# First layer: the first query's product in the round of NSA's compression, and the memories' squares summed on GpSimd

## The chip, the cores and the metric

One core of one Trainium2 chip runs the whole program. The metric is the device time of one execution, in microseconds. Below, "products" are dense matrix products on TensorE, and "the remainder" of a weight is its low part, explained further down.

## What is computed

Two transformer blocks follow each other on 512 tokens of width 1024, in float32. The first block (`first_block`) is the one that the change is about:

```python
h = rms_norm(x, norm_in_g[l])
p = h @ w_in[l]                                  # rwkv | nsa | memory columns
y_rwkv = rwkv7_group(p_rwkv, ...)                # 8 heads of 64
y_nsa = nsa_group(p_nsa, pos, ...)               # 4 heads: compressed, selected, window
kv = rms_norm(mem, mem_norm_g[l]) @ w_mem_kv[l]
y_mem = memory_group(p_mem, mem_k, mem_v, ...)   # attention on 256 memory rows
x = x + concatenate([y_rwkv, y_nsa, y_mem]) @ w_out[l]
```

In `nsa_group` the keys and values `kcv` are cut in 31 windows of 32 rows, a position term is added, and a two-layer net compresses each window. Queries and the other keys are rotated (RoPE). The second block has an even mixer, an odd mixer, two cross attentions on another memory of 256 rows (`rms_norm(mem) @ wkv`, 16 column blocks each) and two MLPs.

## The kernel before, in words

**Products.** Activations lie transposed, 128 features by 512 tokens. A weight comes in units of 1024 rows by 128 columns, 512 KB. Each is split in a rounded part, made by ScalarE (`weight_hi`, L165), and a remainder, made by VectorE (`weight_lo`, L171, 1024 columns, it needs the rounded part). The activations are split the same way (L213, L218). `dense` (L189 and on) does 24 matmuls of 512 columns per unit. There are four raw buffers and three split ones: ScalarE prepares two units ahead of the one that is consumed, VectorE one ahead, in the order in which TensorE consumes units. SP loads unit n when the remainder of unit n-4 exists.

**The order of work.** Each engine has its own in-order program, written as generators. `first_layer` (L1437) weaves three lanes: rwkv 0 then rwkv 1; NSA, its heads 0 and 1, then rwkv 2 and 3 together; and, beside NSA, the memory and its heads. In one round each lane takes one step, rwkv first, then NSA, then memory. Each engine does its own part of each step, in this order, so whatever stands behind a waiting instruction on an engine waits too. Rounds are counted from 0:

- round 0: rwkv 0's key product; NSA's `kcv` product; the memory's first four tiles are split and squared
- round 1: LoRA products; NSA's compression, 64 matmul calls (128 instructions) of 64x31, on `kexp`, which VectorE builds by two adds (L1196) from the evacuated `kcv`; the memory's last four tiles
- round 2: the square sum kn of rwkv's key; NSA's q0 product; the memory's first key product, then the statistics of its norm. On VectorE the decay chain of rwkv stands ahead of NSA's step: two sigmoid forms, a scan, centring and differences (L956 to L975)
- round 3: rwkv's receptance product; rotation of q0, the compression's second layer (`c2`), q1's product; the second memory key
- rounds 4 and 5: one product by rwkv, one by NSA with the rotation of the one before, and a memory value
- later: NSA's gates, scores and heads; rwkv's inverse (masked products, six levels) and its four chunks. rwkv 2 and 3 begin at round 40; the layer has 76 rounds.

**Norm statistics.** ScalarE squares a tile (L226), VectorE adds it to a sum (L233); a matmul with ones sums over partitions. ScalarE rounds and squares in turns; the squares go through two buffers, so that from the fourth square on it waits for the addition two before (`square`, L222). For the memories a tile has 256 columns. In the cross layers `keys_vector` (L2023) has all eight tiles in one step, between the evacuation of one pair of query products and the next remainder. GpSimd is idle there; in the first layer it does six multiplies for each rwkv group (`rwkv_pool`).

Of the kernel before, what the change touches and what calls it, by code (L numbers as in the profile page):

```python
# [13 lines left out]
T = 512  # L14
# [206 lines left out]

def square(K, a, name, i, src, acc, tmp, scale=1.0):  # L222

    if i >= 3:
        a.wait_ge(*K.done("dve", *name, "sum", i - 2))
    a.activation(tmp[i % 2] if i else acc, src, ACT.Square, scale=scale).then_inc(*K.tell("act", *name, "sq", i))  # L226


def add_square(K, v, name, i, acc, tmp):
    v.wait_ge(*K.done("act", *name, "sq", i))  # L230
    if i:
        v.wait_ge(*K.own("dve"))
        v.tensor_tensor(acc, acc, tmp[i % 2], ALU.add).then_inc(*K.tell("dve", *name, "sum", i))  # L233


def stats_tensor(K, M, pe, name, acc, n=T, last=7, ones="ones"):
    b = K.take(*name, "ss")
    pe.wait_ge(*K.clear(*name, "ss"))
    if last:
        pe.wait_ge(*K.done("dve", *name, "sum", last))  # L240
# [245 lines left out]
def memory_split_scalar(K, M, a, name, mem, gname, hi, acc, tmp, which=range(ND)):  # L486
    for i in which:
        a.wait_ge(*K.landed(f"mem{i}", name[1] + 1))
        split_hi(K, M, a, name, i, mem[i], hi[i], M.PV(gname, i))
        square(K, a, name, i, mem[i], acc, tmp)  # L490


def memory_split_vector(K, M, v, name, mem, gname, hi, lo, acc, tmp, which=range(ND)):
    for i in which:
        split_lo(K, M, v, name, i, mem[i], hi[i], lo[i], M.PV(gname, i))
        add_square(K, v, name, i, acc, tmp)


def memory_tensor(K, M, pe, name, wname, n, hi, lo, acc, tmp):
    first = True  # L500
    for a in range(0, n, 2):
        for u in (a, a + 1):
            dense(K, M, pe, (*name, "k", u), wname, u, hi, lo, n=256, fresh=name if first else None)
            if first:
                stats_tensor(K, M, pe, name, acc, 256)
            first = False
# [95 lines left out]
def first_memory_vector(K, M, v):  # L602
    g = M.first
    for part in (range(4), range(4, ND)):
        memory_split_vector(K, M, v, M0, g.mem, "mem_norm_g", g.mem_hi, g.mem_lo, g.mem_acc, g.mem_tmp, part)
        yield
    yield from memory_vector(K, M, v, M0, 2, g.kap, g.mem_R, g.mem_vtmp)


def first_memory_scalar(K, M, a):  # L610
    g = M.first
    for part in (range(4), range(4, ND)):
        memory_split_scalar(K, M, a, M0, g.mem, "mem_norm_g", g.mem_hi, g.mem_acc, g.mem_tmp, part)
        yield
    yield from memory_scalar(K, M, a, M0, 2, g.vap, g.mem_R)
# [522 lines left out]
def nsa_tensor(K, M, pe):  # L1138
    s, hi, lo = M.nsa, M.hi[0], M.lo[0]
    dense(K, M, pe, ("kcv",), "w_in", 23, hi, lo)  # L1140
    yield
    pe.wait_ge(*K.landed("w1", 5))
    for z in range(2):
# [9 lines left out]
    yield  # L1153
    before = None
    for key, u, src in (("q0", 17, s.q[0]), ("q1", 18, s.q[1]), ("ks", 24, s.ks), ("kw", 25, s.kw), ("vsw", 26, s.tmp2)):
        if before is not None:
            rope_tensor(K, M, pe, *before)
        if key == "q1":
            b = K.take("c2")
# [27 lines left out]
def nsa_vector(K, M, v):  # L1187
# [5 lines left out]
    for half in range(2):  # L1193
        windows = s.kcv[:, half * 16:half * 16 + 496].rearrange("p (b r) -> p r b", b=31)
        pos = M.PV("pos", half * 16, 16).unsqueeze(2).to_broadcast([128, 16, 31])
        v.tensor_tensor(s.kexp[:, half * 496:half * 496 + 496].rearrange("p (r b) -> p r b", r=16), windows, pos,  # L1196
                        ALU.add).then_inc(*K.tell("dve", "kexp"))
    v.wait_ge(*K.done("pe", "cmp"))
    for z in range(2):
# [5 lines left out]
    K.also("dve", "cmp", 1, "silu")  # L1205
    before = None
    for key, src, dst in (("q0", s.q[0], s.qr[0]), ("q1", s.q[1], s.qr[1]), ("ks", s.ks, s.ks), ("kw", s.kw, s.kw),
                          ("vsw", s.tmp2, None)):
        if key == "q1":
            v.wait_ge(*K.landed("ncs", 2))  # L1210
        if before is not None:
            rope_vector(K, v, *before, s.cos, s.sin, s.tmp)
        if key == "q1":
            b = K.bank("c2")
# [56 lines left out]
def nsa_scalar(K, M, a):  # L1271
    s = M.nsa
    weight_hi(K, M, a)
    yield
    for z in range(2):
        silu_scalar(K, a, ("cmp", z, "h"), s.h[z][0:64, 0:31], s.h[z][0:64, 32:63])
    yield
    for key in ("q0", "q1", "ks", "kw", "vsw"):
        weight_hi(K, M, a)
# [733 lines left out]
def keys_vector(K, M, v, n, r):  # L2013
    s = M.cross
    queries_vector(K, M, v, n, 0, ("n", 2 + 3 * n))
    yield
    memory_split_vector(K, M, v, ("m", n + 1), s.mem, f"xa_mem{n}", M.mem_hi[1 - r], M.mem_lo[1 - r], s.acc, s.sq)
    queries_vector(K, M, v, n, 1)
# [212 lines left out]
def first_norms(K, M, v):  # L2231
    return (chain(idle(12), *(chain(idle(1), head_norms(K, v, nsa_heads(M, z)), idle(3)) for z in range(2))),
            chain(idle(6), *(chain(idle(1), head_norms(K, v, mem_heads(M, z)), idle(3)) for z in range(2))))
# [174 lines left out]
def build(nc, dram):  # L2408
    with ExitStack() as ctx:
# [19 lines left out]
        def halves(ts):  # L2429
# [19 lines left out]
            ("hi", 8), ("lo", 12)))  # L2449
        stats, g.mem_tmp = halves([tile("mem_stats", plain(1, 10))]), halves([tile("mem_sq", plain(1, 11))])  # L2450
        g.mem_acc, g.mem_R = stats
# [253 lines left out]
```

## Time and profile before

| | us |
|---|---|
| timed executions | 2149.06, 2160.72, 2165.86 |
| their median | 2160.72 |
| the profiled execution | 2146.59 |
| its span, first to last instruction | 2145.3 |
| TensorE busy in it | 2020.0 (94%) |
| VectorE, ScalarE, GpSimd busy | 1100.1, 872.5, 57.3 |

All durations below are of the profiled execution, and a sum made from them stands against its own time. The granted clock is a share of TensorE's full 2.4 GHz; 0.50 is the lower level, 1.2 GHz. A row of the timeline has start, length, engine, line, operation, output and inputs, and in brackets how long the engine had been idle and what released it. A length is that of the instruction; followers on the same engine can start before it ends. Engines: PE is TensorE, DVE VectorE, ACT ScalarE, POOL GpSimd.

### The profile page before, as it was taken

What the parts mean: (1) busy time and instruction counts of PE and PEld (TensorE: products, weight loads), DVE (VectorE), ACT (ScalarE), POOL (GpSimd) and SP (SyncE); (2) the same over time, 40 slices, a digit from 0 to 9 for tenths busy, and PEclk for the clock granted to TensorE, in tenths of its full rate; (3) what the DMA queues carried; (4) which work ended last, traced back from release to release, by engine and by line L of the source; (5) the groups of instructions that cost most, each with busy time, mean ns of one, the idle gap of its engine ahead of it and who ended that gap; (6) DMA issues with size and microseconds to landing.
All of it is one profiled execution on the core that took longest, in us unless ns stands there. A gap on an engine that the chain in (4) does not pass through costs nothing.

```text
span 2145.3 us, 28300 instructions
## 1 busy us (share of the span) xinstructions
PE 2020.0 (94%) x11400; PEld 1605.7 (75%) x11400; DVE 1100.1 (51%) x1921; ACT 872.5 (41%) x1567; POOL 57.3 (3%) x92
## 2 busy tenths in 40 slices
PE   6898888889999989999999999999999999999997
PEld 4776566768766669878888887667668978888886
DVE  5567567746466464454334344444565445343344
ACT  5325533244345354343223233565654344232232
POOL 0100012000000000000000000111000000000000
PEclk8989999999999999999999999999999999999999
DMA  5210011013211033222232322111123312322221
GB/s 203 88 50 21 20 59 49 3 60 112 79 59 40 20 118 128 69 89 99 89 105 91 98 99 79 60 50 60 49 79 120 107 59 96 101 98 89 99 98 69
DMA packets 54099, 169.63 MB, mean 79 GB/s; under 512 B 5777, under 2 KB 9425, under 8 KB 53969
## 3 DMA queue, kind: packets, MB, share of 16 engines
q1 hardware_dynamic: 53968, 167.82, 23.4%
q8 instruction: 92, 1.51, 0.3%
q14 instruction: 39, 0.31, 0.0%
HBM read 165.70 MB, written 2.10 MB: 78 GB/s over the span
## 4 chain that ended last, share of the span: by engine, by line
PE 62%; DVE 3%; ACT 2%; issue 1%; DMA 0%; SPq 0%; POOL 0%; DVEq 0%; ACTq 0%
PE ps L152 61%; PE ps L157 1%; DVE lo L1459 0%; DVE wr L171 0%; DVE X L1540 0%; DVE acc L233 0%; DVE X L1613 0%; DVE macc L233 0%; ACT hi L213 0%; ACT sa_sp L2195 0%; ACT sa_sp L2193 0%; ACT sb_sp L2195 0%; DMA raw<-d_sb_w_out 0%; ACT sb_sp L2198 0%; ACT wr L165 0%
## 5 line engine op out<-in xcount | busy, mean ns | idle before, releaser
L152 PE MATMUL ps<-hi,wr 128*128 128x512 f32 (+1 forms) x4616 | 1410.8, 385 | 52.1 <-DVE wr L171 34.7
L152 PEld LDWEIGHTS ps<-hi,wr 128*128 128x128 f32 x4616 | 861.4, 190 | 236.9 <-DVE wr L171 26.9
L152 PE MATMUL ps<-lo,wr 128*128 128x512 f32 (+1 forms) x2308 | 879.9, 381 | 0.0
L152 PEld LDWEIGHTS ps<-lo,wr 128*128 128x128 f32 x2308 | 439.1, 190 | 82.9 <-issue 3.4
L165 ACT ACTIVATE wr<-raw 128x1024 fp32r<-128x1024 f32 x293 | 307.8, 1053 | 360.4 <-PE ps L152 352.1
L171 DVE TENSOR_TENSOR wr<-raw,wr 128x1024 fp32r<-128x1024 f32 x293 | 361.2, 1233 | 4.3 <-ACT wr L165 2.3
L1524 DVE TENSOR_TENSOR X<-X,ps 128x512 f32<-128x512 f32 x80 | 55.0, 687 | 213.5 <-PE ps L152 213.5
L2078 ACT ACTIVATE mlp<-mlp 128x512 f32<-128x512 f32 x64 | 40.4, 632 | 208.1 <-DVE mlp L2061 208.1
L2061 DVE SCALAR_TENSOR_TENSOR mlp<-ps,R 128x512 f32<-128x512 f32 x64 | 44.3, 692 | 113.5 <-PE ps L152 106.5
L2064 DVE TENSOR_TENSOR lo<-mlp,hi 128x512 fp32r<-128x512 f32 x64 | 44.3, 692 | 87.5 <-ACT hi L2082 87.5
L213 ACT ACTIVATE hi<-X,pv 128x512 fp32r<-128x512 f32 x48 | 34.6, 721 | 98.8 <-DVE X L1524 78.4
L218 DVE SCALAR_TENSOR_TENSOR lo<-X,pv,hi 128x512 fp32r<-128x512 f32 x48 | 36.0, 749 | 32.1 <-ACT hi L213 32.1
L226 ACT ACTIVATE sq<-X 128x512 f32<-128x512 f32 x49 | 30.3, 618 | 28.9 <-DVE X L1524 28.9
L2082 ACT ACTIVATE hi<-mlp 128x512 fp32r<-128x512 f32 x64 | 40.4, 632 | 2.4
L233 DVE TENSOR_TENSOR acc<-acc,sq 128x512 f32<-128x512 f32 x50 | 34.6, 692 | 10.3 <-ACT sq L226 5.6
L432 ACT ACTIVATE x_pr<-ps,st 128x256 f32<-128x256 f32 x32 | 15.2, 475 | 60.6 <-DVE st L418 60.6
L2217 POOL TENSOR_SCALAR_AFFINE_SELECT sa_sp<-sa_sp 128x128 f32<-128x128 f32 x24 | 9.8, 409 | 1063.8 <-DVE sa_sp L2159 1063.8
L274 DVE SCALAR_TENSOR_TENSOR Y<-ps,R 128x512 f32<-128x512 f32 x16 | 11.1, 692 | 51.4 <-PE ps L152 48.1
L152 PE MATMUL ps<-x_pt,vt 128*128 128x128 f32 x256 | 34.3, 277 | 2.6 <-ACT x_pt L443 2.6
L152 PEld LDWEIGHTS ps<-x_pt,vt 128*128 128x128 f32 x256 | 32.3, 191 | 5.2 <-ACT x_pt L443 4.3
L152 PE MATMUL ps<-kt,Y 128*128 128x256 f32 x128 | 32.6, 379 | 0.0
L1459 DVE TENSOR_TENSOR lo<-Y,hi 128x512 fp32r<-128x512 f32 x40 | 24.7, 684 | 12.4 <-ACT hi L1453 12.4
(701 smaller groups left out, 1925.1 us busy)
## 6 DMA issues: line engine op xcount, KB each, us to landing
raw<-d_w SPq DMA_DIRECT2D x128, 512.0 KB, 3.4
raw<-d_wkv SPq DMA_DIRECT2D x32, 512.0 KB, 3.5
raw<-d_w_in SPq DMA_DIRECT2D x30, 512.0 KB, 3.5
raw<-d_sb_w_in SPq DMA_DIRECT2D x24, 512.0 KB, 3.4
raw<-d_ev_w_in SPq DMA_DIRECT2D x16, 512.0 KB, 3.5
raw<-d_wq SPq DMA_DIRECT2D x16, 512.0 KB, 3.5
raw<-d_wo SPq DMA_DIRECT2D x16, 512.0 KB, 3.4
X<-d_xT SPq DMA_DIRECT2D x16, 256.0 KB, 5.2
```

What stands on the lines that cost most here:

```text
L152: return pe.matmul(out, lhsT, rhs, start=start, stop=stop, skip_group_check=True)
L165: a.activation(M.wr[u % 3][:, 0:1024], M.raw[u % 4], ACT.Copy).then_inc(*K.tell("act", "hi", u))
L171: v.tensor_tensor(w[:, 1024:2048], M.raw[u % 4], w[:, 0:1024].bitcast(F32), ALU.subtract).then_inc(*K.tell("dve", "lo", u))
L213: a.activation(hi, src, ACT.Copy, scale=gcol).then_inc(*K.tell("act", *name, "hi", i))
L218: v.scalar_tensor_tensor(out=lo, in0=src, scalar=gcol, in1=hi.bitcast(F32), op0=ALU.mult, op1=ALU.subtract).then_inc(*K.tell("dve", *name, ...
L226: a.activation(tmp[i % 2] if i else acc, src, ACT.Square, scale=scale).then_inc(*K.tell("act", *name, "sq", i))
L233: v.tensor_tensor(acc, acc, tmp[i % 2], ALU.add).then_inc(*K.tell("dve", *name, "sum", i))
L1524: v.tensor_tensor(M.X[u], M.X[u], K.bank(*key, u), ALU.add).then_inc(*K.tell("dve", *key, u, frees=(*key, u)))
L2061: v.scalar_tensor_tensor(out=t, in0=K.bank(*key), scalar=0.0, in1=M.R, op0=ALU.max, op1=ALU.mult).then_inc(*K.tell("dve", *key, frees=key))
L2064: v.tensor_tensor(lo[u], t, hi[u].bitcast(F32), ALU.subtract).then_inc(*K.tell("dve", "h", n, q, "lo", u))
L2078: a.activation(t, t, ACT.Square).then_inc(*K.tell("act", *key, "sq"))
L2082: a.activation(hi[u], t, ACT.Copy).then_inc(*K.tell("act", "h", n, q, "hi", u))
```

## The change

Four things. (1) NSA's q0 product moves from round 2 to round 1, ahead of the compression's matmuls; q0's rotation and q1's product go to round 2, and every later NSA step, its heads, and rwkv 2 and 3 stand one round earlier. `c2` stays in round 3. (2) In the first layer's memory ScalarE does all eight roundings and then all eight squares in round 0, and VectorE does the eight remainders in round 1, behind `kexp` and a weight's remainder and ahead of q0's evacuation. (3) All sums of memory squares, here and in both cross layers, are added by GpSimd, at the front of its program, between rwkv's and the odd layer's operations, and at its end. The remainders stay on VectorE. (4) The first memory's squares go through four buffers in place of two; in the cross layers there are still two.

```diff
-def square(K, a, name, i, src, acc, tmp, scale=1.0):
-    if i >= 3:
-        a.wait_ge(*K.done("dve", *name, "sum", i - 2))
-    a.activation(tmp[i % 2] if i else acc, src, ACT.Square, scale=scale).then_inc(*K.tell("act", *name, "sq", i))
+def square(K, a, name, i, src, acc, tmp, scale=1.0, adds="dve"):
+    if i > len(tmp):
+        a.wait_ge(*K.done(adds, *name, "sum", i - len(tmp)))
+    a.activation(tmp[i % len(tmp)] if i else acc, src, ACT.Square, scale=scale).then_inc(*K.tell("act", *name, "sq", i))
...
-def memory_split_vector(K, M, v, name, mem, gname, hi, lo, acc, tmp, which=range(ND)):
+def memory_split_vector(K, M, v, name, mem, gname, hi, lo, which=range(ND)):
     for i in which:
         split_lo(K, M, v, name, i, mem[i], hi[i], lo[i], M.PV(gname, i))
-        add_square(K, v, name, i, acc, tmp)
+def memory_pool(K, g, name, acc, tmp):
+    for i in range(ND):
+        add_square(K, g, name, i, acc, tmp, "pool")
...
 def first_memory_vector(K, M, v):
     g = M.first
-    for part in (range(4), range(4, ND)):
-        memory_split_vector(K, M, v, M0, g.mem, "mem_norm_g", g.mem_hi, g.mem_lo, g.mem_acc, g.mem_tmp, part)
-        yield
+    yield
+    yield
...
 def first_memory_scalar(K, M, a):
     g = M.first
-    for part in (range(4), range(4, ND)):
-        memory_split_scalar(K, M, a, M0, g.mem, "mem_norm_g", g.mem_hi, g.mem_acc, g.mem_tmp, part)
-        yield
+    for i in range(ND):
+        a.wait_ge(*K.landed(f"mem{i}", 1))
+        split_hi(K, M, a, M0, i, g.mem[i], g.mem_hi[i], M.PV("mem_norm_g", i))
+    for i in range(ND):
+        square(K, a, M0, i, g.mem[i], g.mem_acc, g.mem_tmp, adds="pool")
+    yield
+    yield
...
     dense(K, M, pe, ("kcv",), "w_in", 23, hi, lo)
     yield
+    dense(K, M, pe, ("q0",), "w_in", 17, hi, lo)
     pe.wait_ge(*K.landed("w1", 5))
...
-    before = None
-    for key, u, src in (("q0", 17, s.q[0]), ("q1", 18, s.q[1]), ("ks", 24, s.ks), ("kw", 25, s.kw), ("vsw", 26, s.tmp2)):
-        if before is not None:
-            rope_tensor(K, M, pe, *before)
-        if key == "q1":
+    before = ("q0",), "rot_n", s.q[0], K.done("dve", "q0")
+    for key, u, src in (("q1", 18, s.q[1]), ("ks", 24, s.ks), ("kw", 25, s.kw), ("vsw", 26, s.tmp2)):
+        rope_tensor(K, M, pe, *before)
+        if key == "ks":
...
+    weight_lo(K, M, v)
+    g = M.first
+    memory_split_vector(K, M, v, M0, g.mem, "mem_norm_g", g.mem_hi, g.mem_lo)
+    evac(K, M, v, ("q0",), s.q[0], R)
     v.wait_ge(*K.done("pe", "cmp"))
...
     weight_hi(K, M, a)
     yield
+    weight_hi(K, M, a)
     for z in range(2):
         silu_scalar(K, a, ("cmp", z, "h"), s.h[z][0:64, 0:31], s.h[z][0:64, 32:63])
...
 def first_norms(K, M, v):
-    return (chain(idle(12), *(chain(idle(1), head_norms(K, v, nsa_heads(M, z)), idle(3)) for z in range(2))),
+    return (chain(idle(11), *(chain(idle(1), head_norms(K, v, nsa_heads(M, z)), idle(3)) for z in range(2))),
...
 def pool_program(K, M, g):
+    memory_pool(K, g, M0, M.first.mem_acc, M.first.mem_tmp)
     for i in range(4):
         rwkv_pool(K, g, i, M.rwkv[i])
+    memory_pool(K, g, ("m", 1), M.cross.acc, M.cross.sq)
     sb_layer(M, lambda z, L: sb_pool(K, g, z, L))
+    memory_pool(K, g, ("m", 2), M.cross.acc, M.cross.sq)
```

## Rows read from the trace of the kernel before

**Rows 1.** The page's engine line, then stages: length, busy, granted clock, DMA, GB/s.

```profile
PE 2020.0 (94%) x11400; PEld 1605.7 (75%) x11400; DVE 1100.1 (51%) x1921; ACT 872.5 (41%) x1567; POOL 57.3 (3%) x92
...
20.00:66.00 46.00, 37.43 (x243) 29.68 (x244) 27.48 (x61) 22.59 (x41) 0.00 (x0) 0.78 0.33 110
...
110.00:480.00 370.00, 325.11 (x3312) 245.32 (x3310) 237.45 (x534) 151.79 (x326) 21.79 (x18) 0.95 0.11 38
...
780.00:1600.00 820.00, 802.14 (x3803) 638.24 (x3802) 376.96 (x588) 351.37 (x610) 27.09 (x64) 0.99 0.25 83
```

**Rows 2.** Stages of TensorE alone in rounds 1 to 3: length, busy, granted clock.

```profile
36.50:41.40 4.90, 0.01 (x2) 0.71 0.00 2
41.40:48.40 7.00, 6.98 (x129) 0.50 0.01 2
48.40:56.80 8.40, 8.40 (x28) 0.77 0.01 2
56.80:59.70 2.90, 0.02 (x2) 0.89 0.00 0
59.70:65.40 5.70, 5.70 (x26) 0.50 0.36 113
65.40:71.10 5.70, 5.70 (x25) 0.96 0.46 152
```

**Rows 3.** Timeline of VectorE in rounds 0 to 2.

```profile
32.13 1.22 DVE L171 TENSOR_TENSOR wr<-raw,wr 128x1024 fp32r<-128x1024 f32 x1
35.49 0.69 DVE L277 TENSOR_TENSOR nsa_kcv<-ps,R 128x512 f32<-128x512 f32 x1 [2.14 <-PE ps L152]
...
39.39 1.89 DVE L1196 TENSOR_TENSOR nsa_kexp<-nsa_kcv,pv 128x496 f32<-128x496 f32 x2
...
53.19 0.42 DVE L956 TENSOR_SCALAR ra_sg<-ra_sg 128x512 f32<-128x512 f32 x1
...
58.38 1.21 DVE L171 TENSOR_TENSOR wr<-raw,wr 128x1024 fp32r<-128x1024 f32 x1
```

**Rows 4.** Timeline of TensorE: kn, and 32 small matmuls at either clock.

```profile
48.38 2.07 PE L152 MATMUL ps<-ra_tmp,cst 128*128 128x512 f32 x2
...
154.98 1.13 PE L152 MATMUL ps<-ra_Z,ra_X 64*64 64x64 f32 x32
...
159.21 0.69 PE L152 MATMUL ps<-ra_T,ra_S 64*64 64x64 f32 x32
```

**Rows 5.** Timeline of VectorE and GpSimd while both work.

```profile
79.45 2.05 DVE L171 TENSOR_TENSOR wr<-raw,wr 128x1024 fp32r<-128x1024 f32 x1
80.38 1.71 POOL L1112 TENSOR_TENSOR ra_kr<-ra_kk,ra_Sx 128x256 f32<-128x256 f32 x1
...
82.05 0.73 POOL L1114 TENSOR_TENSOR ra_kr<-ra_r,ra_S 128x256 f32<-128x256 f32 x1
...
82.21 1.66 DVE L171 TENSOR_TENSOR wr<-raw,wr 128x1024 fp32r<-128x1024 f32 x1
```

**Rows 6.** Cross layers: VectorE and TensorE's timeline at 790, then TensorE's stages.

```profile
788.77 0.87 DVE L218 SCALAR_TENSOR_TENSOR lo<-mem,pv,hi 128x256 fp32r<-128x256 f32 x2
...
795.65 1.22 DVE L171 TENSOR_TENSOR wr<-raw,wr 128x1024 fp32r<-128x1024 f32 x1
...
797.01 0.77 PE L152 MATMUL ps<-hi,wr 128*128 128x512 f32 x1 [3.44 <-DVE wr L171]
...
797.00:805.50 8.50, 8.49 (x25) 0.64 0.39 125
1624.20:1629.70 5.50, 5.50 (x25) 1.00 0.54 190
```

**Rows 7.** Rounds of rwkv 2 and 3: TensorE's waits, VectorE's timeline, a stage.

```profile
PE ps L152 <- DVE wr L171: 14.3, 3, 4.9
...
325.07 0.69 DVE L277 TENSOR_TENSOR ra_g<-ps,R 128x512 f32<-128x512 f32 x1 [3.21 <-PE ps L152]
...
341.79 1.21 DVE L171 TENSOR_TENSOR wr<-raw,wr 128x1024 fp32r<-128x1024 f32 x1
...
343.00:349.00 6.00, 5.85 (x14) 0.50 0.25 87
```

More of the change, by code:

```diff
@@ L219, in split_lo, with add_square, stats_tensor @@
                            op1=ALU.subtract).then_inc(*K.tell("dve", *name, "lo", i))
-def square(K, a, name, i, src, acc, tmp, scale=1.0):
-    if i >= 3:
-        a.wait_ge(*K.done("dve", *name, "sum", i - 2))
-    a.activation(tmp[i % 2] if i else acc, src, ACT.Square, scale=scale).then_inc(*K.tell("act", *name, "sq", i))
-def add_square(K, v, name, i, acc, tmp):
+def square(K, a, name, i, src, acc, tmp, scale=1.0, adds="dve"):
+    if i > len(tmp):
+        a.wait_ge(*K.done(adds, *name, "sum", i - len(tmp)))
+    a.activation(tmp[i % len(tmp)] if i else acc, src, ACT.Square, scale=scale).then_inc(*K.tell("act", *name, "sq", i))
+def add_square(K, v, name, i, acc, tmp, adds="dve"):
     v.wait_ge(*K.done("act", *name, "sq", i))
     if i:
-        v.wait_ge(*K.own("dve"))
-        v.tensor_tensor(acc, acc, tmp[i % 2], ALU.add).then_inc(*K.tell("dve", *name, "sum", i))
-def stats_tensor(K, M, pe, name, acc, n=T, last=7, ones="ones"):
+        v.wait_ge(*K.own(adds))
+        v.tensor_tensor(acc, acc, tmp[i % len(tmp)], ALU.add).then_inc(*K.tell(adds, *name, "sum", i))
+def stats_tensor(K, M, pe, name, acc, n=T, last=7, ones="ones", adds="dve"):
     b = K.take(*name, "ss")
@@ L239, in stats_tensor @@
     if last:
-        pe.wait_ge(*K.done("dve", *name, "sum", last))
+        pe.wait_ge(*K.done(adds, *name, "sum", last))
     else:
@@ L489, in memory_split_scalar @@
         split_hi(K, M, a, name, i, mem[i], hi[i], M.PV(gname, i))
-        square(K, a, name, i, mem[i], acc, tmp)
-def memory_split_vector(K, M, v, name, mem, gname, hi, lo, acc, tmp, which=range(ND)):
+        square(K, a, name, i, mem[i], acc, tmp, adds="pool")
+def memory_split_vector(K, M, v, name, mem, gname, hi, lo, which=range(ND)):
     for i in which:
         split_lo(K, M, v, name, i, mem[i], hi[i], lo[i], M.PV(gname, i))
-        add_square(K, v, name, i, acc, tmp)
+def memory_pool(K, g, name, acc, tmp):
+    for i in range(ND):
+        add_square(K, g, name, i, acc, tmp, "pool")
 def memory_tensor(K, M, pe, name, wname, n, hi, lo, acc, tmp):
@@ L504, in memory_tensor @@
             if first:
-                stats_tensor(K, M, pe, name, acc, 256)
+                stats_tensor(K, M, pe, name, acc, 256, adds="pool")
             first = False
@@ L1205, in nsa_vector @@
     K.also("dve", "cmp", 1, "silu")
[L1206 to L1213, printed above, removed]
+    v.wait_ge(*K.landed("ncs", 2))
+    before = ("q0",), s.q[0], s.qr[0]
+    for key, src, dst in (("q1", s.q[1], s.qr[1]), ("ks", s.ks, s.ks), ("kw", s.kw, s.kw), ("vsw", s.tmp2, None)):
+        rope_vector(K, v, *before, s.cos, s.sin, s.tmp)
+        if key == "ks":
             b = K.bank("c2")
@@ L1277, in nsa_scalar @@
     yield
-    for key in ("q0", "q1", "ks", "kw", "vsw"):
+    for key in ("q1", "ks", "kw", "vsw"):
         weight_hi(K, M, a)
@@ L2016, in keys_vector @@
     yield
-    memory_split_vector(K, M, v, ("m", n + 1), s.mem, f"xa_mem{n}", M.mem_hi[1 - r], M.mem_lo[1 - r], s.acc, s.sq)
+    memory_split_vector(K, M, v, ("m", n + 1), s.mem, f"xa_mem{n}", M.mem_hi[1 - r], M.mem_lo[1 - r])
     queries_vector(K, M, v, n, 1)
@@ L2449, in build @@
             ("hi", 8), ("lo", 12)))
-        stats, g.mem_tmp = halves([tile("mem_stats", plain(1, 10))]), halves([tile("mem_sq", plain(1, 11))])
+        stats, g.mem_tmp = halves([tile("mem_stats", plain(1, 10))]), halves([tile("mem_sq0", plain(1, 11)), tile("mem_sq1", plain(1, 13))])
         g.mem_acc, g.mem_R = stats
```

## The prediction

> **What bounds the kernel now.** The page comes first: TensorE is busy 94% of the span [rows 1], so a change pays only where TensorE stands still, runs at the lower clock, or gets less to do. Then the table by stages: the first layer's opening, 20 to 66 us, has 37.4 us of TensorE work in 46 us at a mean granted clock of 0.78; from 780 us on the kernel is nearly full [rows 1]. The opening is where this change works, so the next view is its table cut at TensorE's events [rows 2]. Read it as a story: 4.9 us of nothing, 7.0 us of compression matmuls at 0.50 (1.2 GHz), the square sum and q0's product while the clock comes back, 2.9 us of nothing, the first memory key at 0.50, and only at 65.4 the next product. VectorE's rows say who was late [rows 3]: kcv was evacuated at 35.5, but the two adds that build kexp start at 39.4 behind seven operations of the memory's first half; and the weight remainder for the memory key starts at 58.4 behind the decay chain that starts at 53.2. Last, in each of the two cross layers TensorE waits 3.4 us for a remainder, which stands behind fifteen memory operations, eight remainders and seven additions [rows 6].
>
> **Part 1, the order of the first rounds.** I follow TensorE from 36.5, when the two LoRA products end.
>
> q0's product needs weight unit 3, whose remainder was written from 32.1 on (1.22 us) [rows 3], so it starts at once and runs at the full clock: 5.7 us by the row 65.4 to 71.1 [rows 2], to 42.2. That fills the 4.9 us gap. VectorE meanwhile does kexp directly behind kcv: 36.2 plus 1.9, and up to 0.5 for each of the two adds if GpSimd stands in the way (part 2), 39.1 at the latest. So the wait for kexp is gone; it was worth 4.9 us, and what is late next is the clock.
>
> The compression: 128 matmul instructions, 7.0 us at 0.50 [rows 2]. There is no row of them at 2.4 GHz. Bounds: the block of 32 matmuls of 64x64 took 1.13 us at the lower clock and 0.69 at the full one [rows 4], so the best is 7.0 x 0.69/1.13 = 4.3; the worst is 7.0. Before, the clock had fallen inside the idle stretch and 7 us of these small matmuls did not bring it back [rows 2]; now they start at full clock and may lose it on the way. I take the middle, 5.6, ending at 47.8.
>
> Then kn and the rotation of q0 (kn took 2.1 at the lower clock [rows 4], so 1.1 at the full one; taken 1.6 each): 51.0. The rotation needs q0's evacuation on VectorE. In VectorE's queue that stands behind kexp, one remainder (1.2) and eight memory remainders (0.44 apart, 3.5): about 44 without, 46 with GpSimd's interference, hidden under the compression. q1's product needs unit 4, remaindered by then: 51.0 to 56.7, or 57.5 with a cold start.
>
> The memory key's product needs unit 5. Its remainder stands on VectorE behind: compression end 47.8, the copies 0.3, the decay chain with the two SiLUs 5.2 (53.2 to 58.4 in [rows 3]), and now also the rotation's three operations, 512 columns each like kcv's evacuation (2.1 together, formerly a round later). So it starts at 55.4 and ends at 56.6, and q1's product ends between 56.7 and 57.5: the 2.9 us gap closes, by little. The key's product with the statistics took 5.7 at 0.50 [rows 2]; at full clock about half, 2.9, with 0.6 for filling: from 57.1 to 60.7, against 65.4, a gain of 4.7. With a compression of 4.3 it is VectorE that is late (46.5 + 0.3 + 5.2 + 2.1 + 1.2 = 55.3, key done at 58.8, gain 6.6). With one of 7.0 and the cold 8.4 us for kn and a product that [rows 2] show, plus 2.1: 59.7, key done at 63.2, gain 2.2.
>
> At that point TensorE has also done a product and a rotation that used to come after it: 5.7 + 1.0 = 6.7 us less for the rest. All later NSA steps and heads stand one round earlier against rwkv 0 and 1, rwkv 2 and 3 likewise, and the layer has 75 rounds instead of 76. Rounds 3 to 5 keep their shape (a product by rwkv, one by NSA, one by the memory). Behind them the alignment changes: the rounds of the inverse are latency chains that NSA's matmuls fill, and the 6.7 us are kept only where TensorE is the late one. From 110 to 480 the layer has 45 us of idle TensorE in 370 [rows 1], 12%, and stalls shift rather than add. I keep 4.7 of the 6.7; bounds: nothing and all of it. One place I worked through, since the largest stalls are there, three waits for a remainder, 14.3 us in sum [rows 7]. Before, VectorE's queue between the gate's evacuation (325.1) and the wanted remainder (341.8) [rows 7] is 2.5 of masks, 9.1 of both decay chains, and 2.5 of masks; TensorE covers it with LoRA, kn, masked products and one product whose weights are ready. After, only one block of masks lies in that queue (2.5 less) but also one block of four products (2.2) and the LoRA pair (2.0) less of cover. It comes out 1.7 longer or so at one place, and this is inside the 2.0 I wrote off.
>
> ScalarE: its eight roundings and eight squares now stand together in front of kk2 and the two tanh. From 30.7: 8 x 0.40 + 8 x 0.33 = 36.5 without waits, 38.4 if the last squares wait for GpSimd; their reader is VectorE's decay chain, in round 2, no sooner than 46.5. Costed at nothing; if that cover were gone it would cost its 0.5 us. Loads: SP issues unit n when remainder n-4 exists; these remainders come earlier or at the same place, and the extra memory of the ring is in a tile of its own. Nothing is moved past a wait on SP.
>
> Part 1: 4.7 + 4.7 = 9.4 us, bounds 2.2 and 13.3.
>
> **Part 2, the squares' sums on GpSimd.** 21 additions of 128x256 leave VectorE (0.42 each, 0.44 in the queue) and go to GpSimd, where multiplies of this size took 0.73 alone and 1.71 beside VectorE [rows 5]. The rows show what the two do to each other. VectorE's remainder at 79.45 took 2.05 and that at 82.21 took 1.66 instead of 1.22; GpSimd's operation at 80.38 took 1.71 and ended 0.6 behind the end of VectorE's. While either works on two SBUF operands the other stands still. The Trainium skill, "GPSIMD Engine Reference", section 8 (Key points), says the same of instructions with two SBUF inputs; by that, and by these rows, the moved additions are not free to VectorE. Its section 4.1 (Engine selection) advises VectorE for elementwise adds, GpSimd being about two times slower; by that factor an addition would be 0.85 instead of the row's 0.73, and the sum below would change by some tenths.
>
> Cross layer, per layer [rows 6]: ScalarE's squares begin 3 us and more before VectorE is free for them, at 785, so GpSimd's chain can start at 786.2, well before VectorE's first memory remainder at 788.77 (it waits for a product's end). At 0.75 to 0.8 each, three to three and a half additions are done by then; the others alternate with VectorE's eight remainders. A turn of GpSimd costs VectorE what the lock costs beyond the overlap of dispatch, 0.45 to 0.5 (the remainder at 82.21 lost 0.44 to one addition-sized operation). New length of the block: 3.5 + 0.4 + 3 x 0.5 = 5.4, against 795.65 - 788.77 = 6.9: 1.5 us off a stall of 3.4. Bounds: 0.3 (GpSimd at 1.71 for each, sums queued behind, ScalarE's last rounding late) and 3.4 (all the stall). ScalarE's squares still wait, now for GpSimd; its last rounding is out by 791, before VectorE wants it. What is late next is the same remainder, 1.5 earlier.
>
> The clock: behind the stall at 797 the product took 8.5 us at 0.64, behind the equal one at 1624 it took 5.5 at 1.00 [rows 6]. So the stall costs 3.0 more in one of two cases; with a stall of 2 us instead of 3.4 I count half of that as saved: 1.5, bounds 0 and 3.0. Both layers: 2 x 1.5 + 1.5 = 4.5; bounds 0.6 and 9.8. TensorE is nearly full behind both stages [rows 1], so this carries to the end. In the first layer the same additions are hidden: they are wanted by the statistics at about 60 us and are done by 45.
>
> **Sum.** 9.4 + 4.5 = 13.9 us off the profiled execution's 2146.6 (span 2145.3), which gives 2132.7. That execution was the quickest of the four known; the three timed ones have the median 2160.7. On that scale the forecast is 2160.7 - 13.9 = 2146.8.
>
> **Rivals.**
> - *The gain sticks at part of the opening* (chance 0.20). The port exclusion takes back what VectorE was relieved of (0.6 left), and the earlier NSA lane finds rounds that wait for VectorE or ScalarE anyway, so the 6.7 us are not kept: 4.7 + 0.6 = 5.3, 2155.4. For it: the 1.71 rows, and 12% idle in the layer. Against it: half of the additions run before VectorE comes, and NSA's steps are products, the thing that TensorE is late with in rounds 3 to 5. The skill's advice of section 4.1 would point here.
> - *Everything goes well* (0.12). The compression keeps the full clock, all 6.7 us are kept (13.3), both cross stalls close and the clock with them (9.8): 23, 2137.6.
> - *Slower* (0.06). In the rounds where rwkv 2 and 3 run their decay chains together, VectorE is the late one. If the new alignment leaves the first of the two products there without a ready remainder, TensorE stands 5.6 us longer, and the next six run at 0.50 as at 343 [rows 7], some 3 us more: 8.6 for each of three such places, 25.8 in all, 12 us slower, 2172.6. It decides from the second place on (two cost 17.2, more than 13.9). Against it: each consumer prepares the next unit's remainder, so the first product is ready in either order.
>
> **How the numbers follow.** The forecast has 0.62. Its own range, with the mid-bounds of both parts, is a gain of 8 to 19 us, 2142 to 2153. The timed executions of before lie 17 us apart, so the median of a few moves by some 5 us, and with the first two rivals in, the range is 2132 to 2160. One per cent is 21.6 us, about what a measurement of this kernel can tell from no change. A gain beyond it needs the good case, or the forecast with the scatter's help: 0.22. Slower by over it: the last rival, partly: 0.03. Within: 0.75.
>
> **What would show it.** Right: q0's product directly behind the LoRA products at about 36.5 with no gap; kexp starting near 36.2; the first memory key's product starting at 57 to 58 and the product after it at 60 to 62; seven GpSimd adds per stage, beginning near 35, and lengthened ones among them; VectorE's eight memory remainders in the cross layers in 5 to 6 us, TensorE's wait behind them 1.5 to 2.5. Wrong: a clock of 0.50 through the compression and q1 (part 1 down to 2.2), adds of 1.71 throughout, a first layer that ends less than 6 us sooner although round 3 begins 11 us of work ahead, or longer waits for a remainder in the rounds of rwkv 2 and 3.

## The result, and the profile after

The changed kernel took 2126.7 us, median of 4 runs (2118.0 to 2129.6), beside 2158.2 of the kernel before (4 runs, 2149.1 to 2165.9). The ratio is 0.986, 95% interval 0.9835 to 0.9886: 30 us or 1.4% less. The forecast of 2146.8 was 20 us too high, and the time lies 5 us below the range's low end of 2132. The profiled executions are only 17 us apart, 2146.6 and 2129.6.

First the changed kernel's engine line and the three stages of [rows 1] (busy time of TensorE, weight load, VectorE, ScalarE and GpSimd, granted clock, DMA share, GB/s).

```profile
PE 2017.5 (95%) x11400; PEld 1599.8 (75%) x11400; DVE 1096.6 (52%) x1900; ACT 874.4 (41%) x1569; POOL 75.2 (4%) x113
...
20.00:66.00 46.00, 43.76 (x302) 33.37 (x302) 34.23 (x66) 25.86 (x45) 7.03 (x7) 1.00 0.41 140
110.00:480.00 370.00, 327.54 (x3307) 245.53 (x3306) 239.27 (x537) 159.80 (x338) 22.25 (x18) 0.94 0.12 42
780.00:1600.00 820.00, 802.78 (x3812) 638.83 (x3811) 378.93 (x585) 350.91 (x605) 27.93 (x67) 1.00 0.25 83
```

In the opening TensorE is busy for 43.8 us in place of 37.4, and all of it at the full clock, in place of 0.78. The second row holds the start of the output stage, which before came after 480, so idle time has to be compared up to a fixed event, as below. GpSimd has 21 more instructions, VectorE 21 fewer.

TensorE's timeline in rounds 1 to 3, to be read against [rows 2]:

```profile
41.03 0.39 PE L152 MATMUL ps<-hi,wr 128*128 128x512 f32 x1
41.35 3.92 PE L152 MATMUL ps<-nsa_kexp,cmp_w 64*64 64x31 f32 x128
45.20 1.12 PE L152 MATMUL ps<-ra_tmp,cst 128*128 128x512 f32 x2
46.16 1.02 PE L152 MATMUL ps<-nsa_q,cst 128*128 128x512 f32 x2
...
54.16 0.36 PE L152 MATMUL ps<-memhi,wr 128*128 128x256 f32 x1 [1.50 <-DVE wr L171]
```

q0's product ends at 41.4 and the compression follows with no gap. It takes 3.92 us, against 6.98, and keeps the full clock. The memory key starts at 54.2 (before 59.7) behind a wait of 1.5 (before 2.9). Its statistics are at 57.1, against 65.0, and the next product starts at 57.4, against 65.4. Over three traces of either kernel the mean starts of that product are 57.6 and 64.7, 7.1 us apart.

VectorE and GpSimd in the same rounds; see [rows 3]:

```profile
35.44 2.39 DVE L1204 TENSOR_TENSOR nsa_kexp<-nsa_kcv,pv 128x496 f32<-128x496 f32 x2
37.75 1.72 DVE L171 TENSOR_TENSOR wr<-raw,wr 128x1024 fp32r<-128x1024 f32 x1
39.39 4.69 DVE L218 SCALAR_TENSOR_TENSOR memlo<-mem,pv,memhi 128x256 fp32r<-128x256 f32 x8
44.19 0.69 DVE L277 TENSOR_TENSOR nsa_q<-ps,R 128x512 f32<-128x512 f32 x1
...
52.84 1.22 DVE L171 TENSOR_TENSOR wr<-raw,wr 128x1024 fp32r<-128x1024 f32 x1
...
33.93 7.89 POOL L233 TENSOR_TENSOR mem_stats<-mem_stats,mem_sq 128x256 f32<-128x256 f32 x7 [33.42 <-ACT mem_sq L226]
```

kexp starts directly behind kcv. GpSimd's seven additions take 7.9 us, 1.13 each, and VectorE pays beside them: kexp 2.39 (before 1.89), a remainder 1.72 (before 1.22), eight memory remainders 4.69 (0.44 apart they would be 3.5). That is 2.2 us in all, hidden under q0's product and the compression: the evacuation of q0 still ends before the compression.

The cross layers, to be read against [rows 6]: GpSimd, VectorE and TensorE in the first, TensorE in the second.

```profile
774.82 6.24 POOL L233 TENSOR_TENSOR macc<-macc,msq 128x256 f32<-128x256 f32 x7 [432.04 <-ACT msq L226]
...
777.34 5.19 DVE L218 SCALAR_TENSOR_TENSOR lo<-mem,pv,hi 128x256 fp32r<-128x256 f32 x8
...
782.45 1.21 DVE L171 TENSOR_TENSOR wr<-raw,wr 128x1024 fp32r<-128x1024 f32 x1
...
783.81 0.47 PE L152 MATMUL ps<-hi,wr 128*128 128x512 f32 x1 [1.68 <-DVE wr L171]
...
783.50:792.00 8.50, 8.19 (x47) 1.00 0.40 125
...
1608.78 0.47 PE L152 MATMUL ps<-hi,wr 128*128 128x512 f32 x1 [1.75 <-DVE wr L171]
```

VectorE's memory block is 5.2 us long, and the wait behind it 1.7, where it was 3.4. GpSimd has begun its chain 2.5 us before VectorE is free.

Between 110 and 480 TensorE's waits for a remainder, against the 14.3 us in three of [rows 7]: the sum, its count and longest, then the four of them.

```profile
PE ps L152 <- DVE wr L171: 9.5, 4, 4.2
...
279.89 0.47 PE L152 MATMUL ps<-hi,wr 128*128 128x512 f32 x1 [0.87 <-DVE wr L171]
286.37 0.47 PE L152 MATMUL ps<-hi,wr 128*128 128x512 f32 x1 [0.75 <-DVE wr L171]
...
321.08 0.47 PE L152 MATMUL ps<-hi,wr 128*128 128x512 f32 x1 [4.24 <-DVE wr L171]
...
339.63 0.77 PE L152 MATMUL ps<-hi,wr 128*128 128x512 f32 x1 [3.62 <-DVE wr L171]
```

Before, the three were 4.5, 4.9 and 4.8 us (at 304.6, 343.2 and 362.8). The first has shrunk to two of less than 1 us, the others by 0.7 and 1.2.

**Where the 26 us between traces are.** Three executions of either kernel were traced. The table cuts them at the same events; "idle" is TensorE's idle time, "low" the time at 1.2 GHz worked out from the granted clock, read in steps of 5 us, both means of three.

```
stage                              length        idle          low
                                before after  before after  before after
0 to 110 us                      110.0 110.0    24.4  18.0    22.7   5.7
110 to first residual add        383.0 361.1    46.7  43.0    55.7  41.0
to the first cross layer         268.5 271.6    15.3  15.3    14.6  21.4
first cross layer                164.0 160.0     9.0   7.3     7.0   1.4
feed-forward and odd layer       685.1 685.3     9.8   9.9     3.4   3.4
second cross layer to last add   529.3 525.9     8.7   7.0     4.5   2.3
```

The first layer ends 21.9 us sooner (493.0 and 471.1), the cross layers give 4.0 and 3.4, and 3.1 are given back before the first of them, with the same idle time and 6.8 us more at the lower clock. That loss is probably a matter of single executions: the same stretch had 23.4 low microseconds in one trace of the kernel before and 10.2 in the other two, and 10.3 and 20.4 in the two traces of one and the same variant further down; but all three traces of the changed kernel have 20.5 to 23.2. In the profiled pair the first layers are 17.7 and the cross layers 6.1 apart, and 6.8 of that is lost in the stretches between, so that it ends 17 apart.

**How far single executions explain themselves.** Each timed execution comes with its mean granted clock, hence with its microseconds at the lower clock. A straight line through all 151 timed executions, with one constant for each kernel and one slope for all, gives a slope of 0.37 (standard error 0.01): a microsecond at 1.2 GHz cost 0.37 of time. The constants are what each kernel would take with none.

```
kernel              n   mean us   low us   constant (error 1.0 to 1.3)
before             70    2154.9    117.0   2111.9
order only          6    2138.9     95.6   2103.7
squares only       12    2142.2     95.4   2107.1
after              16    2126.8     82.2   2096.6
lane not shifted    6    2132.7     89.6   2099.8
before, warmed     12    2151.6    108.0   2111.9
before, cross fill 12    2149.9    106.8   2110.6
after, early cross  6    2120.4     76.4   2092.3
after, early both  11    2120.1     81.0   2090.3
```

By this line 28.1 us part the two kernels: 15.3 in the constant (the table of stages has 13.5 us less idle), and 12.8 for 35 us less at the lower clock. The difference of two constants has an error of 0.6 to 1.0, less than each of them. The second part is an inference from a fit; no run changed the clock alone over the whole kernel.

### The profile page after: what moved, and what is told of

The parts are those of the page before. It is cut to its first block, busy times and chain, and to the rows that moved or that the text cites. A ratio compares the mean times of both kernels' runs of the same rounds, so it can differ in the third digit from the quotient of the medians.

```text
span 2128.4 us, 28299 instructions
## 1 busy us (share of the span) xinstructions
PE 2017.5 (95%) x11400; PEld 1599.8 (75%) x11400; DVE 1096.6 (52%) x1900; ACT 874.4 (41%) x1569; POOL 75.2 (4%) x113
## 4 chain that ended last, share of the span: by engine, by line
PE 62%; DVE 3%; ACT 2%; issue 1%; DMA 0%; SPq 0%; POOL 0%; DVEq 0%; ACTq 0%
PE ps L152 61%; PE ps L157 1%; DVE lo L218 1%; DVE lo L1469 0%; DVE wr L171 0%; DVE acc L233 0%; ACT hi L213 0%; DVE X L1550 0%; DVE X L1623 0%; DMA raw<-d_ev_w_out 0%; DMA raw<-d_sb_w_out 0%; ACT sa_sp L2205 0%; ACT sa_sp L2203 0%; ACT sb_sp L2205 0%; ACT sb_sp L2208 0%
```

## The experiments

The median of before differed between the three groups of runs (2158.0, 2151.6, 2150.7), so each ratio is against the runs of its own group.

**The kernels again.** The kernel before, unchanged: 

> The kernel before once more, for a second trace of it and more times. The pair of profiled executions differs by 17.0 us, the medians by 31. Theory A (the first trace of before was a lucky one): this execution's span is 2150 to 2160, the first memory key or the compression or another stretch shows more time at 0.50, and the extra time lies in the clock, not in new waits. Theory B (the changed kernel's gain is only 17 and the earlier median was unlucky): its median is near 2147 and the ratio of the changed kernel to it in this call about 0.992.

 Measured: 2158.1, ratio 1.0006 (0.9985 to 1.0026). Its trace has 143 low microseconds (span 2162.2 at 0.967), where the first profile had 99 (2145.3 at 0.977), with every wait of the opening, the inverse's rounds and the cross layers as in [rows 2], [rows 6] and [rows 7]. The forecast's own base, 2146.6, was an execution with few of them.

The changed kernel, twice: 

> The changed kernel again beside the others. Theory A expects 2120 to 2130 and a ratio to before of 0.984 to 0.989; Theory B about 0.992. If parts add up: order only plus squares only equals this gain within 4 us; the stage up to the first residual of the first layer ends near 472.

 

> The changed kernel once more, to stand beside e10 on one chip and for a third trace. Pooled over its executions so far the mean is 2126 with 80 us at the lower clock; 2120 to 2131 here. The compression at 3.9 us and the first 66 us wholly at the full clock, as in both earlier traces; between 110 us and the first residual 40 to 46 us at the lower clock if that stretch is a lottery with this mean.

 Measured: 2129.0, ratio 0.9868 (0.9842 to 0.9894), and 2129.3, ratio 0.9877 (0.9854 to 0.9900). With the 0.986 of the first comparison that is a gain of 26 to 30 us each time. The kernel before a third time: 

> A third trace of the kernel before. If the time at the lower clock between 110 us and the first residual is a lottery, it lies between or near the 45 and 72 us of the other two traces, and the even mixer has either 0 or about 13 us of it; waits are the same as in the others within 3 us in every stage.

 It gave 2151.2 and the third trace of the table.

**One part at a time.** The order alone is the kernel before with part (1) of the change: the memory keeps its two halves, in rounds 0 and 1, and every sum stands on VectorE behind its remainder, as this excerpt of the difference from the changed kernel shows:

```diff
-def memory_split_vector(K, M, v, name, mem, gname, hi, lo, which=range(ND)):
+def memory_split_vector(K, M, v, name, mem, gname, hi, lo, acc, tmp, which=range(ND)):
     for i in which:
         split_lo(K, M, v, name, i, mem[i], hi[i], lo[i], M.PV(gname, i))
+        add_square(K, v, name, i, acc, tmp)
```

> Only the order is changed: q0's product in round 1, everything of NSA one round earlier, the memory's two halves and all additions as before. My part 1 sum: 9.4 us off before. If the first rounds gained by the order alone: compression under 4.5 us at the full clock, wait for kexp gone although kexp starts at 39.4 again, the first memory key about 8 us sooner than 59.7, the first layer's end 15 us or more sooner than 489.5, total 18 to 25 us faster than before. Rival: the memory block on VectorE had to be moved too, then the gain of this kernel is under 8 us.

Measured: 2141.1, ratio 0.9923 (0.9898 to 0.9948), 16.6 us less, where 18 to 25 were expected. The key starts at 58.1 and not 8 us sooner than 59.7, and the first layer ends at 472.5, 17.0 sooner than 489.5.

The squares alone are the kernel before with parts (3) and (4).

> Only the additions of the memories' squares go to GpSimd (with four buffers in the first memory), the order of the first rounds as before, the two halves too. My part 2 sum: 4.5 us faster, 1.7 off each cross stall (3.4 to 1.7) and the clock with it; kexp starts about 1.3 sooner than before in the first layer since three additions are gone from VectorE, less what GpSimd takes of the port. Rival (the port takes back all): within 2 us of before.

Measured: 2140.5, ratio 0.993 (0.991 to 0.995), 15.1 us less, far more than the 4.5 expected. Together they have 31.7, where the changed kernel, run beside them, has 28.5: within the intervals they add. By the constants it is 8.2 for the order, 4.8 for the squares and 15.3 for the whole change. The 2.3 (error 1.0) between belong to part (2), the memory block in one piece, and to what the parts do to each other. Part (2) has no run of its own.

The two timelines of the opening tell why either is worth much there. First TensorE with the order alone, then with the squares alone.

```profile
40.74 3.92 PE L152 MATMUL ps<-nsa_kexp,cmp_w 64*64 64x31 f32 x128
...
58.07 0.55 PE L152 MATMUL ps<-memhi,wr 128*128 128x256 f32 x1 [6.01 <-DVE wr L171]
```

```profile
39.32 7.04 PE L152 MATMUL ps<-nsa_kexp,cmp_w 64*64 64x31 f32 x128 [3.31 <-DVE nsa_kexp L1201]
46.29 2.07 PE L152 MATMUL ps<-ra_tmp,cst 128*128 128x512 f32 x2
...
57.47 0.35 PE L152 MATMUL ps<-memhi,wr 128*128 128x256 f32 x1 [3.17 <-ACT ra_S L1066]
...
60.41 0.59 PE L152 MATMUL ps<-mem_stats,cst 128*128 128x256 f32 x2
```

VectorE with the order alone, and the same start of the decay chain in the changed kernel:

```profile
44.71 0.28 DVE L1202 COPY st<-ps 64x31 f32<-64x31 f32 x2 [2.81 <-PE ps L152]
45.70 0.48 DVE L218 SCALAR_TENSOR_TENSOR memlo<-mem,pv,memhi 128x256 fp32r<-128x256 f32 x1 [0.72 <-ACT memhi L213]
...
49.07 0.42 DVE L233 TENSOR_TENSOR mem_stats<-mem_stats,mem_sq 128x256 f32<-128x256 f32 x1
49.42 0.42 DVE L956 TENSOR_SCALAR ra_sg<-ra_sg 128x512 f32<-128x512 f32 x1
```

```profile
45.52 0.41 DVE L964 TENSOR_SCALAR ra_sg<-ra_sg 128x512 f32<-128x512 f32 x1
```

With the order alone the memory's whole second half, four remainders and four additions with a wait of 0.7 for ScalarE in front, stands in VectorE's queue ahead of the decay chain, which starts at 49.4 and not at 45.5. The key waits 6.0 us, the clock falls (0.55 for its first matmul instead of 0.36), and the statistics come at 62.9. With the squares alone kexp is 2.1 us earlier, the wait before the compression 3.3 instead of 4.9 us, the compression still at the lower clock, but the key at the full one; the statistics come at 60.4. With the whole change they come at 57.1, with none of it at 65.0. These are single traces: in four with the opening of before the statistics lie between 62.8 and 65.0, in five with that of the changed kernel between 56.6 and 57.6. So on top of the order the rest of the change is worth some 5 to 6 us at this event. How much of it the four additions are (4 x 0.42 = 1.7 us in the queue), and how much the remainders that now stand ahead of q0's evacuation, no run separates.

**The shift of the lane.** The changed kernel, with NSA's later steps, heads and rwkv 2 and 3 put back one round; round 1 and 2 keep their new contents.

```diff
         dense(K, M, pe, (key,), "w_in", u, hi, lo)
         yield
+    yield
     turn_tensor(K, M, pe, ("vsw",), s.tmp2)
...
-    return (chain(idle(11), ...
+    return (chain(idle(12), ...
```

> The changed kernel with one idle step in NSA's lane behind vsw, so that gates, scores, heads and rwkv 2 and 3 stand in the rounds of before and the layer has 76 rounds again; rounds 0 to 6 as changed. If the gain comes from the first rounds: within 4 us of the changed kernel. If the earlier lane is what the later rounds profit from, or what changes their clock: 5 to 12 us slower than the changed kernel, the loss lying between 110 us and the first residual; one more round of rwkv 2 and 3 alone at the layer's end is worth 1 to 3 of it.

Measured: 2133.4, ratio 0.9912 (0.9882 to 0.9943), where the changed kernel has 0.9868 and 0.9877; the intervals overlap. The constant is 3.2 us higher (error 0.8). Its waits tell more than its time, TensorE's sum between 110 and 480 and one of the three:

```profile
PE ps L152 <- DVE wr L171: 14.1, 3, 5.0
...
287.57 0.77 PE L152 MATMUL ps<-hi,wr 128*128 128x512 f32 x1 [4.52 <-DVE wr L171]
```

These are the three waits of [rows 7] again. With the lane shifted they are 9.5 us, and the order alone has the 9.5 too. So the new alignment takes 4.6 us of waits away; it does not add 1.7. Idle time from 110 to the first residual add is 48.0 here, 43.0 in the changed kernel, 46.7 in the one before.

**The clock in the opening, by itself.** The kernel before with 20 matmuls that compute nothing wanted ahead of the compression, in the gap of 4.9 us.

```diff
+    for f in range(20):
+        mm(pe, K.bank("cmp", f % 2), hi[0][:, 0:128], hi[f % ND], True, True)
     pe.wait_ge(*K.done("dve", "kexp"))
```

> The kernel before with 20 extra matmuls of 128x512 on TensorE ahead of the compression, into the two banks that the compression then overwrites; nothing else moves. They fill the 4.9 us in which TensorE waits for kexp (20 x 0.227 = 4.5 us). If the clock is what made the compression take 7.0 us and the memory key 5.7, the compression takes 3.9 here, kn 1.1, the rest of the opening starts 3.1 us sooner and, if the clock also holds through the 2.9 us wait, the key takes 3.3: the product after it starts 3 to 6 us sooner than 65.4, total 3 to 8 us faster, though work was only added. Rival (the order alone gave the gain): the compression again near 7 us, total within 2 us of before.

Measured: 2152.1, ratio 0.9999 (0.998 to 1.0018). TensorE's timeline:

```profile
40.66 3.92 PE L152 MATMUL ps<-nsa_kexp,cmp_w 64*64 64x31 f32 x128
44.51 1.13 PE L152 MATMUL ps<-ra_tmp,cst 128*128 128x512 f32 x2
...
55.82 0.55 PE L152 MATMUL ps<-memhi,wr 128*128 128x256 f32 x1 [4.72 <-ACT ra_S L1061]
```

The compression has the full clock and ends 3.9 us earlier, but nothing else is ready: the wait before the key grows from 2.9 to 4.7, the key falls back to the lower clock, and the statistics come at 61.1, 1.7 to 3.9 us earlier than without the filler. Of this the total shows nothing, where 3 to 8 us were expected: its constant is that of the kernel before, and its first layer ends at 489.0, beside 489.5 to 499.2. The interval of the ratio is 4 us wide to either side, so a gain of a few microseconds is not excluded, one like the 16.6 of the order alone is. What the change has besides is a product in the gap.

**The clock behind the cross stalls.** The kernel before with 14 such matmuls in each of the two waits of 3.4 us.

```diff
+    for f in range(fill):
+        mm(pe, out, hi[0][:, 0:128], hi[f % nk], True, True)
     pe.wait_ge(*K.done("dve", "lo", u))
```

> The kernel before with 14 extra matmuls (3.2 us) on TensorE in the stall of each cross layer, into the bank that the next query product then overwrites. No wait is removed. If the stall in the first cross layer costs its 3.0 us beyond its length through the clock, the stage from the last residual of the even mixer to the first of the MLP goes from 163.6-164.4 to about 161 and the query product behind it from 8.5 to 5.5; the second cross layer, which kept its clock, does not change. Total 2 to 3 us faster than before. Rival (the fall of the clock there comes from earlier, not from the stall): the stage stays at 164.

Measured: 2149.4, ratio 0.9986 (0.9965 to 1.0007). TensorE's windows, behind the stall and some 110 us later in the same layer:

```profile
805.50:830.00 24.50, 23.28 (x170) 1.00 0.48 151
...
918.00:924.00 6.00, 4.69 (x11) 0.55 0.01 3
924.00:930.00 6.00, 6.00 (x25) 0.88 0.25 87
```

The query product that had 0.64 [rows 6] now runs at the full clock, yet the layer is as long as it was (163.5, mean before 164.0) and has 7.4 us at the lower clock, beside 6.8 to 7.2 before, only elsewhere. The same kernel without the fill does that as well: in its second trace half of the low time of this layer lies between 924 and 936. In all traces of this layer the clock falls behind one of two stretches in which TensorE waits, this stall or some 3 us of waits 110 us later, behind both, or behind neither. Why it is the one or the other these runs do not show; the rival of the expectation, that the fall comes from earlier, fits the length of the layer but not the query product at the full clock.

**The waits that are left.** Two versions of the changed kernel. In the first the weight's remainder in the cross layers is written ahead of the eight memory remainders; in the second also ahead of the rotation in NSA's steps:

```diff
+    weight_lo(K, M, v)
     memory_split_vector(K, M, v, ("m", n + 1), s.mem, f"xa_mem{n}", M.mem_hi[1 - r], M.mem_lo[1 - r])
-    queries_vector(K, M, v, n, 1)
+    queries_vector(K, M, v, n, 1, early=True)
...
+        weight_lo(K, M, v)
         rope_vector(K, v, *before, s.cos, s.sin, s.tmp)
...
-        weight_lo(K, M, v)
         evac(K, M, v, (key,), src, R)
```

> The changed kernel, but in the cross layers VectorE makes the next weight's remainder ahead of the eight memory remainders instead of behind them. If the last stalls of 1.7 us there are VectorE's queue and nothing else, both vanish: 3.4 us faster than the changed kernel, cross stages 157.5 and 523.5. Rival (the memory block then delays the first evacuation or the memory key): the wait moves behind the query products and the gain is under 1 us.

> As the one before, and in the first layer NSA's steps make the weight's remainder ahead of the rotation. If the waits of 1.50 at 54.2 and 3.04 at 73.3 in the changed kernel are this order: both shrink by 2 us (three operations of 0.69), 3 to 4 us more than the kernel before it in this list, and the clock does not fall at the second wait. Rival (the chain through the rotation is the late one): no change against it.

> Remainders ahead of the memory block and of the rotation, again, beside the changed kernel. From the fit over executions (time = T0 + 0.37 x time at the lower clock) its T0 is 6.6 us lower: 4 to 9 us faster than e9 in the same call.

Measured: 2119.6, ratio 0.9855 (0.9827 to 0.9883); 2119.7, ratio 0.9846 (0.9819 to 0.9874); the second version again 2122.0, ratio 0.9851 (0.9827 to 0.9874), beside 2129.3 of the changed kernel in the same group. The first loses both stalls of 1.7 us; TensorE's idle time in the two stages goes from 7.3 and 7.0 to 5.7 and 5.2, and the constant is 4.3 us lower. The second also loses the 1.5 before the memory key, as VectorE's timeline and TensorE's next wait show:

```profile
50.78 1.21 DVE L171 TENSOR_TENSOR wr<-raw,wr 128x1024 fp32r<-128x1024 f32 x1
52.09 0.69 DVE L1139 TENSOR_TENSOR nsa_qr<-nsa_q,nsa_cos 128x512 f32<-128x512 f32 x1
...
56.46 0.47 PE L152 MATMUL ps<-hi,wr 128*128 128x512 f32 x1 [0.41 <-DVE wr L171]
```

The other wait that was expected to go, 3.0 us before the second memory key at 73.3, is only down to 2.4, though the clock no longer falls there. The second version was to be 3 to 4 us better than the first; their medians are equal, and its constant is 2.0 lower (error 0.9). It is 6.3 us below the changed kernel's, and its ratios to the kernel before are the lowest of all that ran, 32 to 33 us less, though their intervals overlap with the changed kernel's. Within the third group the two medians are 7.3 us apart. So the stalls of the cross layers were a matter of the order in VectorE's queue; taking the additions out halved them, moving one instruction then removed the rest. Whether the moved instruction alone, with the additions still on VectorE, would do as well was not run.

## Why the prediction was wrong, by its steps

The median lies 20.1 us below the forecast. Of this 5.8 are the base: the forecast started from 2160.7, the median of three executions, and the mean of all 70 is 2154.9. The other 14.2 are a gain of 28.1 in place of 13.9, half of them clock (12.8 for 5.7) and half work and waits (15.3 for 8.2).

- **The gap and the compression: right, and under-sized.** Filled gap, kexp behind kcv, key earlier: as told. The lower bound of 4.3 us for the compression, scaled from matmuls of 64x64, was above the measured 3.92, and the middle, 5.6, was no evidence. The rows of rounds 1 to 3 showed the clock falling only where TensorE stood still, so with the gap filled the full clock was the likely value. The next product came at 57.4, forecast 60.7, good case 58.8. This is 8.1 us in the profiled pair and 7.1 in the means of three, instead of 4.7.
- **The write-off of 2.0 of 6.7 us in the later rounds: wrong in sign.** Nothing was lost there; idle time fell by another 3.7. The place worked through was to be 1.7 longer; it came out 0.7 shorter, and all three waits together went from 14.3 to 9.5. The failed term can be read in VectorE's queue, one row of before, then three of after:

```profile
327.86 2.48 DVE L779 TENSOR_TENSOR ra_S<-ps,m 128x512 f32<-128x512 f32 x4 [2.10 <-PE ps L152]
```

```profile
307.57 0.69 DVE L277 TENSOR_TENSOR ra_g<-ps,R 128x512 f32<-128x512 f32 x1 [4.52 <-PE ps L152]
308.18 0.42 DVE L964 TENSOR_SCALAR rb_sg<-rb_sg 128x512 f32<-128x512 f32 x1
...
319.71 1.22 DVE L171 TENSOR_TENSOR wr<-raw,wr 128x1024 fp32r<-128x1024 f32 x1
```

From the gate's evacuation to the wanted remainder the queue is 12.1 us long, against 16.7. The sum took out the block of masks (2.5) but not the 2.1 us that VectorE stood still in front of it, waiting for TensorE; this went with it. So the queue is 4.6 shorter, and the cover some 3.9, near the 4.2 of the sum. The first of the three waits, which the argument for one place did not look at, nearly vanished. With the lane put back the old waits return. The first layer nearly adds up with this: 7.1 in the opening, 6.7 of work done earlier, 3.7 less idle and 14.7 low microseconds less at 0.37 (5.4) are 22.9, against 21.9 measured.
- **VectorE's block and the stall: right.** 5.2 and 5.3 us for 5.4, waits of 1.7 and 1.75 for 1.9. That the engines stand in each other's way was visible again. "GPSIMD Engine Reference" of the Trainium skill, section 4.1 (Engine selection), advises VectorE for elementwise adds, GpSimd being about two times slower. The trace agrees on the durations, 0.9 to 1.1 us each in the chains against 0.42; as advice for this kernel the measurement decides against it, with a ratio of 0.993 for the squares alone, since in the changed kernel's trace TensorE waits for none of these additions.
- **The clock: mis-sized, half of the missing gain.** The sum credited 1.5 us in the cross layers, and in the opening 1.4 for the compression and 2.8 for the key's product, 5.7 in all. Over executions the changed kernel spends 82 us at the lower clock and not 117, worth 12.8 by the fit. The three traces of either kernel, 33 apart, place 17.0 before 110 us, 5.6 in the first cross layer and 14.7 in 110 to the first residual add, where three traces of one kernel lie between 44 and 72; 6.8 are lost again behind it. Why the squares alone lose 21.6 of them stays open: their one trace, with 112 a slow one of its kernel, has 17.1 before 110 us and 3.4 in the first cross layer, 6 and 4 less than the mean before.
- **The scale: wrong.** The sum was made on a profile with 99 low microseconds, while the kernel's mean is 117, and then set against a median of three that was itself 5.8 above the mean. A sum on such a trace leaves out gains in stretches that happened to be undisturbed.
- **The split into parts.** I put the additions of the first layer at nothing, as hidden. In both orders the memory's second half stands ahead of the decay chain and so of the key, and my part 1 had silently taken its additions as gone. The squares alone gave 15.1 us and not 4.5: 4.8 in the constant, where the sum has 3.0 without its clock term, and the rest goes with fewer low microseconds, whose cause stays open.

Of the rivals, "everything goes well" (23 us) was nearest, and it was too small too: it had the full clock in the compression and all 6.7 us kept, but no gain in idle time beyond them. That it came near is in part luck, since it also wanted both cross stalls closed, and they were halved. "Slower" needed a product without a ready remainder in the rounds of rwkv 2 and 3; those waits shrank. "Sticks at the opening" needed the lock of the two engines to reach TensorE; its 2.2 us in the opening were covered.

## What to carry to other kernels

Where a gap on the bounding engine can be filled by work that is due anyway, count the clock with it: filler alone showed no gain, within 4 us, and the order with a product in the same place gave 16.6. When lanes of a software pipeline shift, work through every large wait of the old alignment, or leave zero as the value; one place and a doubt made 5.7 us of error here. Try to put the remainder that TensorE wants next ahead of bulk work in VectorE's queue before moving that work to a slower engine; here it was only run after the move. Compare two kernels by the microseconds at the lower clock of each execution before reading a difference of 1%.

## What the runs showed of the hardware

- Executions of one kernel spread over 20 us (2144 to 2166), and almost all of that follows the microseconds at the lower clock, 0.37 us for each. That is less than the 0.5 that work at half the clock would lose; the clock is also low in part of the time in which TensorE stands still (0.71 in the gap of 4.9 us [rows 2]). 117 and 82 low microseconds at 0.37 are 43 and 30 us, 2.0% and 1.4% of the time, and their difference is nearly half of the gain. The Trainium skill, "TensorE: Matmul & The Clock Gate", Part 1, puts the cost of the clock's ramp below 1% of a typical kernel's span, in a passage on a kernel's start. The falls here lie in mid-run, behind waits, and no run measures the ramp at the start.
- The 128 matmuls of 64x31 hold the level at which they start: 6.98 and 7.04 us at 1.2 GHz, 3.92 in each of the traces in which TensorE came to them busy.
- A fall of the clock that filler removes at one place turned up at another of the same layer, in the one trace of that kernel: 7.4 us in all, beside 6.8 to 7.2 without.
- GpSimd's dependent additions of 128x256 took 0.89 each (6.24 for seven) beside VectorE's eight remainders, and 1.13 in the opening beside its longer two-input operations; VectorE's remainder of 128x256 took 0.65 beside them, 0.44 apart without.
